# A gated linear recurrence cut into 72 pieces and issued inside a chunked scan, its gelu product moved into the merge

## The reference

```
xc = causal_dwconv(xb)                      # 4 taps per channel
rg = sigmoid(block_diag_linear(xc, wa, ba)) # 64x64 blocks
ig = sigmoid(block_diag_linear(xc, wx, bx))
log_a = -8 * rg * softplus(-lam);  a = exp(log_a)
bt = sqrt(-expm1(2 * log_a)) * (ig * xc)
h[t] = a[t] * h[t-1] + bt[t]                # latents start from the context's last h
out = (to_raster(h_fwd + h_bwd) * gelu(gb)) @ w_proj_lru
```

## Time and profile before

| | us |
|---|---|
| median of 3 executions | 4632.7 (4627.71 to 4637.73) |
| profiled execution, its own time | 4621.79 |
| its span | 4619.7 |
| busy: PE | 3646.6 (79%) |
| busy: DVE | 2311.1 (50%) |
| busy: ACT | 1607.4 (35%) |
| busy: POOL | 1109.7 (24%) |

### The profile page before, as it was taken

The page is one execution under the profiler, slowest core; times in us unless marked ns, Lnnn a source line. Parts: engine busy times, 40 slices in busy tenths (PEclk is TensorE's granted clock), DMA queues, the critical chain, the costliest instruction groups (busy, mean ns, idle before and its releaser), DMA issues. The chain is left out here.

```text
span 4619.7 us, 121779 instructions
## 1 busy us (share of the span) xinstructions
PE 3646.6 (79%) x53101; PEld 3222.9 (70%) x53101; DVE 2311.1 (50%) x3662; ACT 1607.4 (35%) x2405; POOL 1109.7 (24%) x1088
## 2 busy tenths in 40 slices
PE   5799999997112777777777778989369999999993
PEld 2678888885001667667676768967269999999992
DVE  3156666402886333333333336543656666666664
ACT  3256665411322122222222215433124444444344
POOL 2223333210000453453443314500001111011110
PEclk8899999998655899999999989999579999999996
DMA  4245555422012332332323127543047667676675
GB/s 162 78 143 178 176 174 177 145 73 72 31 37 78 97 76 73 81 93 74 81 71 78 41 84 226 174 137 128 29 156 211 202 209 209 195 217 201 210 210 198
DMA packets 562442, 610.38 MB, mean 132 GB/s; under 512 B 65618, under 2 KB 466836, under 8 KB 560404
## 3 DMA queue, kind: packets, MB, share of 16 engines
q1 hardware_dynamic: 515604, 492.25, 34.7%
q0 software_dynamic: 21856, 80.75, 6.0%
q10 hardware_dynamic: 24480, 29.72, 2.1%
HBM read 443.09 MB, written 159.40 MB: 130 GB/s over the span
## 5 line engine op out<-in xcount | busy, mean ns | idle before, releaser
L647 PE MATMUL moe_h<-moe_xt_hi,moe_w_hi 128*128 128x256 f32 x2048 | 583.0, 285 | 16.6 <-DVE moe_xt_lo L526 15.0
L526 DVE TENSOR_TENSOR moe_w_lo<-moe_w_lo_whole,moe_w_hi 128x2048 fp32r<-128x2048 f32 (+1 forms) x258 | 453.5, 1758 | 265.7 <-ACT moe_w_hi L704 188.8
L647 PE MATMUL moe_h<-moe_xt_hi,moe_w_lo 128*128 128x256 f32 x2048 | 581.2, 284 | 0.0
L647 PE MATMUL moe_h<-moe_xt_lo,moe_w_hi 128*128 128x256 f32 x2048 | 581.1, 284 | 0.0
L1966 PE MATMUL inward_pp<-u_u_hi,inward_w_hi 128*128 128x512 f32 (+1 forms) x1360 | 528.1, 388 | 20.7 <-POOL inward_w_lo L2126 20.7
L1966 PE MATMUL inward_pp<-u_u_lo,inward_w_hi 128*128 128x512 f32 (+1 forms) x1360 | 516.6, 380 | 0.0
L1966 PE MATMUL inward_pp<-u_u_hi,inward_w_lo 128*128 128x512 f32 (+1 forms) x1360 | 516.2, 380 | 0.0
L647 PEld LDWEIGHTS moe_h<-moe_xt_hi,moe_w_hi 128*128 128x128 f32 x2048 | 394.0, 192 | 29.3 <-issue 25.5
L647 PEld LDWEIGHTS moe_h<-moe_xt_lo,moe_w_hi 128*128 128x128 f32 x2048 | 394.0, 192 | 3.7
L647 PEld LDWEIGHTS moe_h<-moe_xt_hi,moe_w_lo 128*128 128x128 f32 x2048 | 393.9, 192 | 0.0
L1966 PEld LDWEIGHTS inward_pp<-u_u_hi,inward_w_hi 128*128 128x128 f32 x1360 | 257.4, 189 | 79.7 <-POOL inward_w_lo L2126 20.9
(11 more groups left out here) (374 smaller groups left out, 9636.3 us busy)
## 6 DMA issues: line engine op xcount, KB each, us to landing
moe_w_lo_whole<-in_moe_w SPq DMA_DIRECT2D x387, 512.0 KB, 4.9
scratch_ops<-inward_ops SPq DMA_DIRECT2D x72, 514.0 KB, 3.8
scan_over<-scratch_ops SPq DMA_DIRECT2D x72, 512.0 KB, 10.2
inward_w_lo_whole<-in_w_in SPq DMA_DIRECT2D x38, 512.0 KB, 4.5
scan_aq<-scratch_ops SPq DMA_DIRECT2D x36, 516.0 KB, 5.8
scratch_gates<-inward_out SPq DMA_DIRECT2D x64, 256.0 KB, 2.1
all_late<-in_w_mod POOLq DMA_DIRECT2D x16, 1024.0 KB, 8.7
rest_modsum<-scratch_gates SPq DMA_DIRECT2D x64, 256.0 KB, 4.0
```

Of the source, the lines that this page charges most:

```text
L526: return nc.vector.tensor_tensor(x_lo, x, x_hi.bitcast(F32), ALU.subtract)
L647: mm = nc.tensor.matmul(hb[ft % 2][m][:, 0:CAP], w_, x, start=(k == 0 and part == 0), stop=(k == KD - 1 and part == 2))
```

## The change

- The stage `rglru` is gone. Its work is cut into 72 pieces k: 4 tiles of 128 channels, 2 directions, 9 groups of 256 columns (the context first). Piece k goes with chunk `k % 4` of the state steps of body `k // 4`.
- X step: PE multiplies two gate weights with the piece's taps (128x128 by 256 columns, fp32), into the free halves of two of the state's PSUM banks; the signal that X is done stands on the second of these. ACT copies X, then takes two tanh of the gates (sigmoid by tanh). DVE does the series (3 operations) of piece k - 1.
- Z step: ACT computes exp, its square and two linear terms; DVE does three taps of piece k + 1 and the gated input of piece k; POOL makes the mask and 1 - x (two operations). At chunk 0 ACT takes the sqrt of the four pieces of the body before.
- S step: ACT copies the window of piece k + 2 and does its first tap; at chunks 0 and 2 DVE does the recurrence (input, scan, add to z) of two pieces of the body before.
- After the last body: the last series, sqrt, and four recurrences, the store of the last tile of z.
- H has three buffers in place of five, `ob` and `over` have one in place of two (loaded one body ahead, so that body 16 now also holds a load), `w_mod` comes in halves of 512 KB into one buffer, two halves per body.
- `blend` gets z without gelu, loads gb (512 KB per block), and POOL multiplies z by gb ahead of z_lo; ACT's z_hi waits for that.

```diff
+                    k = 4 * it + c
+                    DVt.wait(pe, "t3", k)
+                    pe.wait_ge(s_wbd, 64 * (k // NG + 1))
+                    mm = nc.tensor.matmul(bank[u][0][:, G:2 * G], wbd[:, u, :], xc[:, k % 2, :], start=True, stop=True)
                 elif step == "Z":
...
                 elif step == "S":
                     DVc[u].wait(pe, f"Z{c}", it)
+                    ACg.wait(pe, "ri"[u], 4 * it + c)
...
+            def gated_input(k):
+                x = gated[:, k % RING, :]
+                ACg.wait(dve, "i", k)
+                DVi.did("i", dve.scalar_tensor_tensor(out=x, in0=x, scalar=1.0, in1=xc[:, k % 2, :], op0=ALU.add, op1=ALU.mult))
+
+            def series(k):
+                x = root[:, k % RING, :]
+                ACq.wait(dve, "root", k)
+                DVq.did("q1", dve.tensor_tensor(x, x, la[:, :], ALU.mult))
+                DVq.wait(dve, "q1", k)
+                DVq.did("q2", dve.scalar_tensor_tensor(out=x, in0=x, scalar=1.0, in1=la[:, :], op0=ALU.add, op1=ALU.mult))
+                DVq.wait(dve, "q2", k)
+                POl.wait(dve, "one", k)
+                DVq.did("q3", dve.copy_predicated(x, large[:, :], sq[:, :]))
...
+                    if step == "X":
+                        if k:
+                            series(k - 1)
+                    elif step == "Z":
+                        taps(k + 1)
+                        gated_input(k)
+                    elif c[0] and chunk % 2 == 0:
+                        recur(4 * (c[0] - 1) + chunk)
+                        recur(4 * (c[0] - 1) + chunk + 1)
...
             def begin(i):
                 b = i % 2
+                pool.wait_ge(s_z[b], 16 * (i // 2 + 1))
+                pool.wait_ge(s_gb, 16 * (i + 1))
+                POa.did("z", pool.tensor_tensor(flat(z[b][:, :, :]), flat(z[b][:, :, :]), flat(gb[:, :, :]), ALU.mult))
                 ACa.wait(pool, "zhi", i)
```

More of the change, by code:

```diff
@@ L952, in _ @@
             load_z(1)
+            load_gb(1)
             for i in range(NB):
@@ new lines, in gates @@
+            def gates(k):
+                j, d, m, i = lru_of(k)
+                if k:
+                    ACq.wait(act, "root", k - 1)
+                else:
+                    act.wait_ge(s_cols, 6)
+                ACg.did("r", act.activation(th[:, :], bank[0][0][:, G:2 * G], ACT.Tanh, scale=0.5, bias=lru_col(4, j, d)))
+                if k >= RING:
+                    DVs.wait(act, "scan", k - RING)
+                ACg.did("i", act.activation(gated[:, k % RING, :], bank[1][0][:, G:2 * G], ACT.Tanh, scale=0.5, bias=lru_col(5, j, d)))
+                if k % NG == NG - 1 and k < LAST_PIECE:
+                    load_weights(k // NG + 1)
@@ new lines, in roots, with store_z @@
+            def roots(it):
+                DVq.wait(act, "q3", 4 * it + 3)
+                first = 4 * it % RING
+                for a, e in ([(first, first + 4)] if first + 4 <= RING else [(first, RING), (0, first + 4 - RING)]):
+                    act.activation(root[:, a:e, :], root[:, a:e, :], ACT.Sqrt).then_inc(s_root, 1)
+            def store_z(j):
+                DVs.wait(act, "add", 2 * NG * (j + 1) - 1)
+                act.dma_start(env["z"][j * P:(j + 1) * P, :], z).then_inc(s_z, 16)
@@ new lines, in recur @@
+            def recur(k):
+                j, d, m, i = lru_of(k)
+                x, before = root[:, k % RING, :], root[:, (k - 1) % RING, :]
+                dve.wait_ge(s_root, sum(1 + (4 * it % RING > 2) for it in range(k // 4 + 1)))
+                DVs.did("in", dve.scalar_tensor_tensor(out=x, in0=gated[:, k % RING, :], scalar=0.5, in1=x, op0=ALU.mult, op1=ALU.mult))
+                DVs.wait(dve, "in", k)
+                way = slice(None) if d == 0 else slice(None, None, -1)
+                if m == 0:
+                    start = 0.0
+                else:
+                    start = before[:, G - 1:G] if d == 0 else before[:, 0:1]
+                DVs.did("scan", dve.tensor_tensor_scan(x[:, way], decay[:, k % RING, way], x[:, way], start, ALU.mult, ALU.add))
+                if m == 0:
+                    DVs.did("add", dve.nop())
+                    return
+                DVs.wait(dve, "scan", k)
+                piece = z.rearrange("p (r w) -> p w r", w=GRID_W)[:, 8 * i:8 * i + 8, :]
+                h = x.rearrange("p (w r) -> p w r", r=GRID_H)
+                if d == 0:
+                    if m == 1 and j:
+                        dve.wait_ge(s_z, 16 * j)
+                    DVs.did("add", dve.tensor_copy(piece, h))
+                else:
+                    DVs.did("add", dve.tensor_tensor(piece, piece, h, ALU.add))
@@ L2652, in body @@
                 for m in LEVELS:
+                    if c is None and m == 2:
+                        taps(0)
                     states(f"F{m}", c)
@@ new lines, in _ @@
+            load(0)
+            count = 0
+            for it in range(LAST + 2):
+                more, first = it <= LAST, 4 * (it - 1)
+                if more:
+                    start_solve(it)
+                squares(first)
+                if more:
+                    level(1, it)
+                    level(2, it)
+                squares(first + 1 if it else -1)
+                if more:
+                    level(3, it)
+                    level(4, it)
+                squares(first + 2 if it else -1)
+                if more:
+                    level(5, it)
+                squares(first + 3 if it else -1)
+                if 2 * it < 4 * KD:
+                    for half in range(2):
+                        count = add(2 * it + half, count)
```

468 lines of the change are left out of this document (221 added, 247 removed).

## The result

The changed kernel takes 4377.6 us (median of 4 runs, 4372.7 to 4379.5) against 4630.2 before (4618.2 to 4637.7): ratio 0.9455, interval 0.9433 to 0.9478. The profiled execution took 4372.66 us, its span is 4370.9, 248.8 less than before.

The account below looks back on a forecast made before the run. The prediction took VectorE to bound the recurrence stage and PE's order the scan. Terms -351.8 + 36 + 52 + 5 + 22 + 31 = -206 gave execution 4416, about 4427 us as a median; range 4335 to 4550.

Parts of the forecast that it names:

- Stage removed: The whole recurrence stage ahead of the scan goes away: -351.8 us.
- Gate matmuls: At the end of the scan's X steps: 144 added PE matmuls, half absorbed in PE's pauses, +36 us (0 to 85).
- Rival 1: In the scan, gate matmuls cost nothing and waits 1 us per body: about 4355 us; 20%.
- full price of 72: In the scan, by the skill's instruction-fetch rule no pauses absorb the gate matmuls, so they cost 72 us.
- Waits and tile changes: In the scan's bodies, PE tile changes and new waits between engines cost 3 us per body: +52 us.
- Body 16: In the scan, this body now holds an operand load as the others do: +5 us (0 to 6.6).
- Tail: From last Wf to the merge's first load: longer chunks +13, then series, root, recurrences and store +9; +22 us (10 to 40).
- Merge: In the merge, z_hi waits for POOL's product and delays y, 3.8 us per block: +31 us (0 to 38).
- Rival 3: In the scan, one POOL operation holds up each of 40 added DVE operations per body: slower, about 4745 us; 6%.
- Rival 2: In the scan, in-order waits cost 6 to 10 us per body in place of 3: about 4477 to 4545 us; 22%.

Follow-up runs that it names:

- e6: The kernel before with the changed kernel's scan loads and H buffers, plus one unread 128x256 fp32 matmul per unit and X step: 4653.2 us, ratio 1.0065.
- e4: Changed kernel with only the merge reordered: z_hi behind square, root and tanh on ACT, z_lo behind sum of column tile 3 on POOL: 4348.8 us; repeated, 4346.0.
- g1: Changed kernel without the last two of the three taps at the Z step of chunk 0: 4371.4 us, ratio 0.9460.
- g2: Changed kernel without the last two of the three taps at the Z step of chunk 2: 4368.9 us, ratio 0.9449.
- e2: The kernel before with only the changed kernel's scan loads and H buffers, none of its pieces: 4621.7 us, ratio 0.9982.
- e9: e4 with every piece one body earlier: 4336.6 us, ratio 0.9375; repeated, 4332.6 us.
- e3: Changed kernel with five more 128x256 products on DVE at every Z step, 20 per body, results unused: 4506.4 us, ratio 0.9730.

## Why the prediction was right, and where its sum was off

- **Stage removed, -351.8:** as forecast; nothing of it comes back elsewhere but by the terms below.
- **Gate matmuls, +36 (0 to 85):** right in mechanism; that the size is right, too, is luck. Alone they cost 26 us in the profile and 32 to 38 in the times (e6), with some two thirds of their time in PE's pauses. The price of one was low (0.50 us where it takes 0.63) and the share absorbed was low too (half), and the two errors nearly cancel. Rival 1's free gates fall by e6; its other half, waits of 1 us per body, comes closer than the forecast's 3 (next point). The Trainium skill ("Runtime: NRT & Kernel Launch", Instruction fetch mechanics) says that crossing a block of instructions is mostly hidden. The trace does not agree: 128 of 253 crossings cost over 0.8 us each. The full price of 72 that the prediction took from that rule falls by e6 as well.
- **Waits and tile changes, +52:** the step that was mis-sized. From e6's 1193.7 us to the changed kernel's 1214.5 it is 21 us for everything else that the pieces brought into 17 bodies, 1.2 us per body in place of 3 (with e4's scan, which is the same, 32, and 18 in its repetition). In bodies 1 to 15 alone it is 1.9 (73.35 against 71.41), 1.1 of it busy time of PE (58.3 against 57.2) and 0.9 idle; bodies 0 and 16 are shorter than e6's. The prediction counted 16 tile changes and new waits near its middle; in the changed kernel's profile PE's largest wait in the scan that names another engine than its own stands at 13.3 us for all bodies, where it was 13.0 before:

```profile
PE scan_b L2268 <- DVE scan_W L2596: 13.3, 25, 0.9
```

What the remaining 1.2 us are is open: two of the three taps at chunk 0 or at chunk 2 do not show (g1, g2), the other pieces of DVE's work were not taken out.
- **Body 16, +5:** e2 has 6.6 for it alone, the changed kernel 2.2 (64.9), its scan in e4 and in the repetition 7.6 and 3.4; within the scatter of single bodies that is neither shown nor refuted. **Body 0, not in the sum:** -12.4 (e2). The prediction said that the loads come one body ahead and costed that at nothing; the loads that bunch at the scan's start it did not look at. That is the other part of the miss: with it the bodies' terms would have been 81, not 93.
- **Tail, +22:** 18.8. The four chunks have 8.2 us each by the Z copies (2423.68, 2432.41, 2440.29, 2448.42), 8.1 were forecast; e9 takes the term away.

```profile
2420.86 0.69 DVE L2596 TENSOR_TENSOR scan_Wf<-scan_W,scan_b 128x512 f32<-128x512 f32 x1 [0.30 <-PE scan_b L2268]
...
2423.68 0.73 DVE L2603 COPY scan_Z<-scan_b 128x128 f32<-128x128 f32 x2 [0.86 <-PE scan_b L2349]
...
2448.42 0.48 DVE L2603 COPY scan_Z<-scan_b 128x128 f32<-128x128 f32 x2
...
2462.06 0.32 ACTq L2507 DMA_DIRECT2D scratch_z<-all_late  x1
...
2467.05 0.83 SPq L760 DMA_DIRECT2D all_late<-in_b_mod  x2
```

The series, the root and the four serial recurrences fill the time from 2448 to 2462, the store the rest, 5 us as taken.

- **Merge, +31:** 34.7; the wait per block 3.7 where 3.8 were forecast, 26.0 us of new waits in all where 31 were. The clock's 9.8 us were not in the sum and fill the gap, which is luck. e4 confirms the chain by taking it away.
- **Rival 3 (DVE the bound):** its mechanism is there at the places where POOL is at work (1.43 us per operation in e3), but in the changed kernel it strikes about five operations per body (over 0.3 us longer than the median of their kind), not 40, and there is room for the taps among these (g1). Its price could be had from the kernel before, where the prediction read 0.1 us off a mean of 581 ns: of those 108 operations 19 overlap one of POOL and take 1.05 us, the other 89 take 0.48. **Rival 2** falls: no 6 us per body.

With the bodies at 48 us the forecast would have been 4382, so this one term is nearly all of the 50 us.

## What to carry to other kernels

Work put on engines that wait for a bound one costs what its order costs, not its length: look for the place where the engine idles and its neighbour on the shared ports does too (443 ns or 741 for one operation), and fill that first. A new operation ahead of a short chain (POOL's product ahead of z_hi) should make one move everything behind it in the in-order queue that does not need it: here a reordering gave back 32 us of 35 in the profile, 29 in the times. And count a bound engine's pauses before pricing work on it, and look for what they wait for: here they swallowed some two thirds of the first extra 6 us per body, and less of the next.

## What was not expected of the hardware

- A 128x256 fp32 gate matmul between 64x64 tiles takes 0.63 us of PE's order and one of 16 columns 0.33: about half is there nearly without columns.
- In a row of 64x64 matmuls PE's pauses without a releaser are waits for the next 16,384 bytes of instructions: 128 of 253 blocks cost over 0.8 us, 259 us in all in 1108. They depend on what else is loaded: in body 0 20.4 us with the bunched loads, 12.0 without. PE's idle time shrinks by 4.5 us per body with the first 6.0 us of added matmuls (e6 against e2).
- A wait of 3.7 us per block cost more than itself: the granted clock of a block fell from 1.00 to 0.89 or 0.94 (next blocks), and the merge's 1704 matmuls took 9.8 us longer, 1.4 for each of seven blocks.
